# Issuing the GpSimd low-part subtraction of a weight chunk as two 512-column instructions

## What is computed

```python
u = rmsnorm(h, ln_mix)
x_lru, g_lru, q, k, v = split(u @ w_in)            # 5 x 512 channels
y_lru = rglru(causal_dwconv(x_lru)) * gelu(g_lru)  # conv of 4 taps, gates, scan over tokens
y_att = moba_attention(rmsnorm(q), rmsnorm(k), v)  # 8 heads x 64
h += concat(y_lru, y_att) @ w_out
u = rmsnorm(h, ln_ffn)
g_up, v_up = split(u @ w_up)                       # 2 x 3072 channels
h += (gelu(causal_dwconv(g_up)) * v_up) @ w_down   # conv of 3 taps
h += sigmoid(rmsnorm(h, ln_ple) @ w_ple_gate) * (p @ w_ple_proj)
```

## Time and profile before

| | |
|---|---|
| median of 3 runs | 694.06 us (692.89 to 694.07) |
| the profiled execution, its own time | 692.82 us |
| its span, first to last instruction | 691.0 us |
| TensorE busy | 668.2 us, 97% |
| DVE busy | 401.6 us, 58% |
| ACT busy | 322.6 us, 47% |
| POOL busy | 289.6 us, 42% (110 subtractions: 276.9 us) |
| mean granted TensorE clock | 0.989 |
| share of the chain that ended last | PE 76%, DVE 16%, ACT 3% |

### The profile page before, as it was taken

One profiled execution on the slowest core, in us unless ns is written; L12 is line 12 of the kernel. 1 busy time (PEld: TensorE's weight loads), 2 busy tenths in 40 slices (PEclk: granted clock), 3 DMA queues, 4 the chain that ended last, 5 costly groups with the idle time before them and its releaser, 6 DMA issues.

```text
span 691.0 us, 8732 instructions
## 1 busy us (share of the span) xinstructions
PE 668.2 (97%) x3023; PEld 551.9 (80%) x3023; DVE 401.6 (58%) x515; ACT 322.6 (47%) x461; POOL 289.6 (42%) x127
## 2 busy tenths in 40 slices
PE   6999999899999899999999999999999999999997
PEld 5788888677777688888888888888888888888885
DVE  4686489978994967676676676766631121112033
ACT  6436752666653644645545545464432222224531
POOL 4448443541120536445355364454444444444420
PEclk9999999989999999999999999999999999999999
DMA  8534233110032224342332433433333333233112
GB/s 248 138 92 135 80 91 92 62 61 1 0 88 66 81 78 116 92 121 74 108 103 79 121 91 91 121 91 91 92 92 107 107 91 91 91 97 108 39 46 76
DMA packets 97023, 63.04 MB, mean 91 GB/s; under 512 B 3149, under 2 KB 89833, under 8 KB 97001
## 3 DMA queue, kind: packets, MB, share of 16 engines
q1 hardware_dynamic: 96976, 62.74, 30.7%
q10 hardware_dynamic: 24, 0.01, 0.0%
HBM read 60.64 MB, written 2.10 MB: 91 GB/s over the span
## 4 chain that ended last, share of the span: by engine, by line
PE 76%; DVE 16%; ACT 3%; issue 2%; DMA 1%; SPq 0%; ACTq 0%; DVEq 0%
PE bank L927 25%; PE bank L928 25%; PE bank L929 25%; DVE lx L661 2%; DVE prob L785 2%; DMA xtok<-in_x 1%; DVE prob L773 1%; DVE mixlo L708 1%; DVE lq L704 1%; DVE xclo L672 1%; PE bank L1055 1%; ACT prob L466 1%; DVE ulo L625 1%; DVE lt L702 1%; DVE qtok L732 1%
## 5 line engine op out<-in xcount | busy, mean ns | idle before, releaser
L304 POOL TENSOR_TENSOR wlo<-raw,whi 128x1024 fp32r<-128x1024 f32 x110 | 276.9, 2526 | 369.0 <-ACT whi L352 368.8
L352 ACT ACTIVATE whi<-raw 128x1024 fp32r<-128x1024 f32 x109 | 115.1, 1057 | 151.3 <-PE bank L929 150.6
L927 PE MATMUL bank<-uhi,whi 128*128 128x512 f32 x448 | 176.7, 394 | 4.2 <-DVE ulo L625 4.1
L928 PE MATMUL bank<-ulo,whi 128*128 128x512 f32 x448 | 175.4, 392 | 0.0
L929 PE MATMUL bank<-uhi,wlo 128*128 128x512 f32 x448 | 175.3, 391 | 0.0
L869 DVE SCALAR_TENSOR_TENSOR tmp<-tmp,vec 128x511 f32<-128x511 f32 (+1 forms) x48 | 98.0, 2042 | 34.8 <-ACT tmp L525 31.5
L927 PEld LDWEIGHTS bank<-uhi,whi 128*128 128x128 f32 x448 | 84.9, 190 | 23.1 <-DVE ulo L625 3.5
L929 PEld LDWEIGHTS bank<-uhi,wlo 128*128 128x128 f32 x448 | 84.8, 189 | 17.9
L928 PEld LDWEIGHTS bank<-ulo,whi 128*128 128x128 f32 x448 | 85.0, 190 | 17.6 <-issue 0.2
L927 PE MATMUL bank<-acthi,whi 128*128 128x512 f32 x192 | 74.8, 389 | 0.0
L928 PE MATMUL bank<-actlo,whi 128*128 128x512 f32 x192 | 74.7, 389 | 0.0
(11 more groups left out here) (192 smaller groups left out, 839.8 us busy)
## 6 DMA issues: line engine op xcount, KB each, us to landing
raw<-in_w_up SPq DMA_DIRECT2D x48, 512.0 KB, 3.7
raw<-in_w_down SPq DMA_DIRECT2D x24, 512.0 KB, 3.6
raw<-in_w_in SPq DMA_DIRECT2D x20, 512.0 KB, 3.8
raw<-in_w_out SPq DMA_DIRECT2D x8, 512.0 KB, 3.5
raw<-in_w_ple_gate SPq DMA_DIRECT2D x8, 512.0 KB, 3.7
xtok<-in_x SPq DMA_DIRECT2D x4, 512.0 KB, 5.2
out<-fin SPq DMA_DIRECT2D x8, 256.0 KB, 2.0
raw<-in_w_ple_proj SPq DMA_DIRECT2D x2, 512.0 KB, 3.8
```

Of the source, the lines that this page charges most:

```text
L304: nc.gpsimd.tensor_tensor(wlo[s][:, :], raw[s][:, :], whi[s][:, :].bitcast(F32), ALU.subtract).then_inc(w_lo, 1)
L352: nc.scalar.activation(whi[s][:, :], raw[s][:, :], ACT.Copy).then_inc(w_hi, 1)
L927: mm(o, ahi, bhi, start=start, stop=False)
L928: mm(o, ahi, blo, start=False, stop=False)
```

## The change

The one subtraction of 1024 columns becomes two of 512 columns, one behind the other, with no wait between them. Only the second counts up `w_lo`. It holds for all 110 chunks; the other instructions of POOL and those of all other engines are the same.

```diff
             def lo_part(c, s):
                 pool.wait_ge(w_hi, c + 1)
-                nc.gpsimd.tensor_tensor(wlo[s][:, :], raw[s][:, :], whi[s][:, :].bitcast(F32), ALU.subtract).then_inc(w_lo, 1)
+                nc.gpsimd.tensor_tensor(wlo[s][:, 0:CW // 2], raw[s][:, 0:CW // 2], whi[s][:, 0:CW // 2].bitcast(F32), ALU.subtract)
+                nc.gpsimd.tensor_tensor(wlo[s][:, CW // 2:CW], raw[s][:, CW // 2:CW], whi[s][:, CW // 2:CW].bitcast(F32),
+                                        ALU.subtract).then_inc(w_lo, 1)
```

## The result

The changed kernel takes 683.76 us (median of 4, 683.33 to 684.48) against 693.61 for the kernel before (median of 4). The ratio is 0.9861, with a 95% interval of 0.9845 to 0.9877: by the ratio 9.6 us less, 8.5 to 10.8. The profiled execution took 683.5 us, span 681.7; the span shrank by 9.3 us. The forecast was 687.4, with a range down to 684.2.

What follows compares the result with a forecast made beforehand. TensorE was taken to wait for DVE, which POOL's whole instructions hold up. Terms (a) to (g) summed as 0.3 + 0.3 + 3.5 + 3.9 + 0.3 + 0 - 1.7 = 6.6 us off 694.06: 687.4 us, range 684.2 to 691.2.

Steps and rivals of the forecast that it cites:

- (g): Clock behind TensorE's new idle stretch ahead of `turn_probs(0)`: a fall costing 0 to 3.4 us, taken as 1.7.
- (c): First scores: the wait for `kTlo` and the half clock behind it go, `turn_probs(0)` starts sooner; gain 3.5 us.
- (d): Four attention heads: the last `prob` is held less by POOL's subtraction; gain 3.9 us, bounds 3.5 and 4.9.
- What bounds the kernel, and turns: TensorE waits for DVE; DVE and POOL take turns by whole instructions, a blocked step falling from 2.80 to 1.65 us.
- A half costs 1.22 us, splitting nothing: POOL's subtraction: two halves take 2.44 us where the whole takes 2.41 to 2.47, and DVE gets in between.
- (a): LRU input: each third tap ends 1.2 us sooner, DVE is 4.8 us ahead at the gates; gain 0.3 us.
- (b): q and k: two `lq` products standing alone behind a subtraction end 1.2 us sooner each; gain 0.3 us.
- (e): Behind attention: `acc` ends 1.2 us sooner, the next sum 0.9 later; gain 0.3 us, bounds 0.5 and -0.4.
- (f): MLP and the rest: taps end 1 to 2 us sooner per f, but TensorE never waits there; gain 0.
- the first rival: Clock stays up behind the new gap, or DVE leads the loop: 8.3 or 9.3 us gained, 684.8 to 685.8; chance 0.22.
- That POOL wouldn't give way between its halves: POOL's second half follows too closely, DVE waits for both halves and nothing moves: 694.1 us; chance 0.09.
- Late weights: Second halves wait for whole runs of DVE work, so TensorE waits for low parts: slower, 697.4 us; chance 0.06.

Runs made afterwards that it cites:

- scores_only: Only chunks 20 to 23, beside the four `mixlo` ahead of the first scores, halved, against the kernel before: 689.71 us, ratio 0.9943.
- rest_only: All chunks but 20 to 27 halved, against the kernel before: 692.48 us, ratio 0.9983.
- heads_long_first: Only chunks 24 to 27 split, into 896 and then 128 columns, against the kernel before: 692.05 us, ratio 0.9991.
- heads_only: Only chunks 24 to 27, beside a head's last `prob`, halved, against the kernel before: 688.66 us, ratio 0.9929.
- gap_plus_1: Full change plus one unused DVE reciprocal behind the wait for `exps(0)`, ahead of the first `prob`: 685.51 us, ratio 0.9900 against the kernel before.
- gap_plus_2: Full change plus two unused DVE reciprocals behind the wait for `exps(0)`, ahead of the first `prob`: 685.91 us, ratio 0.9901 against the kernel before.
- quarters: All 110 chunks in four instructions of 256 columns: 680.42 us, ratio 0.9833 against the kernel before.
- quarters_wait_v: All chunks in four pieces, and POOL waits for head 0's four `prob` before v's low parts: 675.70 us, ratio 0.9750 against the kernel before.
- longer_gap: Full change plus one unused DVE reciprocal ahead of head 0's normalise: 683.73 us, ratio 0.9868 against the kernel before.
- eighths: All 110 chunks in eight instructions of 128 columns: 678.50 us, ratio 0.9782 against the kernel before.

## Where the prediction held, and the step that failed

The step that failed is term (g), which took 1.7 us off the gain for a clock that would fall behind TensorE's new idle stretch. The clock didn't fall there, so the term measured 0, and without it the sum was 8.3 us. Of the 1.0 us from there to the 9.3 of the trace, most is in the sizes of (c) and (d), and 0.5 isn't shown to come from the change. What bounds the kernel, and how two engines hold each other, came as forecast.

- **What bounds the kernel, and turns.** Right. TensorE waits for DVE, and DVE for a whole POOL instruction. The step of two taking turns came as 1.70 us against 1.65.
- **A half costs 1.22 us, splitting nothing.** Nearly. It set the step of a half, 1.22, beside the length of a whole instruction, 2.41. From start to start an undisturbed whole one takes 2.37 us, a half 1.25, a quarter 0.70 and an eighth 0.42: about 0.15 us for each instruction beside 2.15 ns a column. The estimate of 0.19 us from the Trainium skill, page GPSIMD Engine Reference, section 3.1, was nearer to this than the nothing that was read from the L331 rows. The halves' extra 0.13 us a chunk made TensorE wait for nothing in the trace.
- **(a)** 0.34 us against 0.3. **(b)** 0.05 against 0.3: what failed there is "two of the products stand alone". Behind `lq` stands the next scan's first product (L701 in the new file), which reads two SBUF tensors too; the second half holds it, 1.78 us instead of 0.68. Counted from the first gate matmul, DVE is 1.14 us ahead when that product starts and 0.04 when it ends, where 2.4 had been worked out.
- **(c)** 3.87 us against 3.5. `kTlo`'s wait and the half clock went as forecast, and scores_only shows that they belong to chunks 20 to 23. The idle stretch ahead of `turn_probs(0)` came as 2.10 us against 2.4. The size is from one trace on each side, and partly luck: with the wait for `kTlo` in place, the stretch from the first scores to `turn_probs(0)` took 13.51, 13.55, 14.03 and 14.34 us in four traces (before, rest_only, heads_long_first, heads_only), the longer the sooner the half clock began. So (c) can be worth up to 0.8 us more.
- **(d)** 4.35 against 3.9, inside its bounds of 3.5 and 4.9. DVE leads the loop more than was taken: the bound of 3.5 counted the waits for `prob` alone, and the waits for `prTlo`, which stood at nothing, gave another 0.8 (1.7 to 0.9).
- **(e)** 0.2 against 0.3, **(f)** 0 as forecast.
- **(g), the term that was mis-sized.** It put a fall of half the largest size into the forecast itself. There was none in any of the four traces with a stretch of 2.10 or 2.11 us there. A fall there costs 1.2 to 1.4 us, by gap_plus_1 and gap_plus_2, and 1.4 in quarters against quarters_wait_v; so both the event and its price were put too high. The reason given for halving the price, idle time in each head, isn't what these traces show: heads 1 to 7 took up nothing (the one at 163 us in scores_only did go into idle time). The rows at hand showed falls behind stretches of 2.6 and 2.97 us between starts, and 2.4 was taken to be alike.
- **The sum.** Without (g) it was 8.3; the trace shows 9.3. Of the difference (c) and (d) hold 0.8, less 0.25 in (b), and 0.5 lies ahead of 26.7 us. That last part isn't shown to come from the change: the same point lies at 25.9 to 27.5 us in kernels that differ only far behind it.
- **The range.** Its lower end, 684.2, was the best rival's 684.8 less 0.6 for the runs. It counted the upper bound of (d) alone and the lower or middle values elsewhere. The kernel before has a median of 692.8 to 694.1 over the four sets of runs here, so the reference of 694.06 was at the upper side of what it does; that part of the miss is chance.
- **Rivals.** What came is the first rival (chance 0.22), with both of its conditions: the clock stayed up and DVE led the loop, 9.3 us. That POOL wouldn't give way between its halves is refuted by the `mixlo` rows. Late weights didn't come with the halves in the trace of the full change. Of the other kernels in halves, one trace has such a wait, at the start, where the others wait for `ulo` (2.02 us between starts instead of 1.76); this is longer_gap:

```profile
PE bank L930 <- POOL wlo L305: 1.7, 1, 1.7
```

With eighths one of 0.85 us stands behind attention.

## What to carry to other kernels

Where two engines hold each other for whole instructions, the length of an instruction on the engine with time to spare is a cost of the critical one: look for instructions on the critical engine that take far longer than their like, and see what stands beside them. Shorter pieces pay where a few held instructions meet a longer run of the other engine's work, and the piece in front of the held one is what counts; moving the work behind the urgent instructions by a wait, with nothing split, paid more still: 6.8 us between head 0 and head 7, where halves gave 4.35. A gain at such a place can carry TensorE's clock with it, so read the granted clock behind each idle stretch before and after, and give the clock a case of its own, not a fixed deduction.

## What was not expected of the hardware

- The subtraction's cost is linear from 1024 down to 128 columns: 0.15 us for each instruction and 2.15 ns a column (2.37, 1.25, 0.70 and 0.42 us between undisturbed starts; the line gives 2.35, 1.25, 0.70 and 0.43).
- A half clock of 3.41 us, nominally a loss of 1.7, cost 1.2 to 1.4 us behind `turn_probs(0)`. Behind `ulo`, up to the `acc` sum, the kernels in halves took 11.18 to 11.65 us with a fall (four traces) and 10.88 without (two). In scores_only, where one began at 163 us ahead of a wait, the stretch from head 0 to head 7 took 57.11 us, as without it.
- Ahead of `turn_probs(0)` the clock fell behind an idle stretch of 2.54 us between starts (one trace) and 3.50 (two), and not behind 2.10 or 2.11 (four). Behind `ulo`, at 2.7 us, it fell in four traces and not in two. Why is open.
- The half clock behind the first scores lasted 6.83 us each time, but the traces in which it began sooner (0.3 instead of 1.5 us behind their start) were up to 0.8 us slower up to `turn_probs(0)`.
